# RWKV core: turning rows and making gates inside the block substitution, four masks moved behind it, one bank for the joins' y

## What is computed

```
def step(state, inp):
    r_t, w_t, k_t, v_t, kk_t, a_t = inp
    sa = jnp.einsum('bhij,bhj->bhi', state, -kk_t)
    state = (state * w_t[:, :, None, :]
             + sa[..., :, None] * (kk_t * a_t)[..., None, :]
             + v_t[..., :, None] * k_t[..., None, :])
    return state, jnp.einsum('bhij,bhj->bhi', state, r_t)
```

## Time and profile before

| what | value |
|---|---|
| runs | 1932.91, 1932.30, 1928.63 us; median 1932.3 |
| span of the profiled execution | 1938.0 us (its whole time is given by this span alone; no separate run time is shown) |
| mean granted PE clock of that execution | 0.981 |
| PE busy | 1867.0 us, 96% |
| DVE busy | 1620.9 us, 84% |
| ACT busy | 1144.5 us, 59% |
| `rwkv_core` in the trace | 574.2 to about 698 us |

### The profile page before, as it was taken

One profiled execution on the slowest core, in us unless ns is written; L12 is line 12 of the kernel. 1 busy time (PEld: TensorE's weight loads), 2 busy tenths in 40 slices (PEclk: granted clock), 3 DMA queues, 4 the chain that ended last, 5 costly groups with the idle time before them and its releaser, 6 DMA issues.

```text
span 1938.0 us, 27277 instructions
## 1 busy us (share of the span) xinstructions
PE 1867.0 (96%) x9408; PEld 1520.5 (78%) x9408; DVE 1620.9 (84%) x1752; ACT 1144.5 (59%) x1146; POOL 323.8 (17%) x336
## 2 busy tenths in 40 slices
PE   7999999999999998999999999999999999999997
PEld 6877777866777877888888888888888888888884
DVE  6877677944567577899999999999999999999996
ACT  4423344235563322577777777777777777777773
POOL 2101110020362510611111111111111111111110
PEclk9999999999997987999999999999999999999998
DMA  8545544041001233999999999999999999999994
GB/s 232 173 140 187 166 148 177 22 120 55 1 18 39 89 112 146 312 347 397 391 397 398 389 397 393 390 391 387 393 393 386 394 382 391 398 386 394 388 367 151
DMA packets 176817, 525.11 MB, mean 271 GB/s; under 512 B 30754, under 2 KB 48242, under 8 KB 176754
## 3 DMA queue, kind: packets, MB, share of 16 engines
q1 hardware_dynamic: 152722, 457.48, 62.2%
q0 software_dynamic: 21952, 66.78, 11.9%
q10 hardware_dynamic: 2080, 0.01, 0.1%
HBM read 499.08 MB, written 25.15 MB: 270 GB/s over the span
## 4 chain that ended last, share of the span: by engine, by line
PE 59%; DVE 2%; issue 0%; POOLq 0%; POOL 0%; DVEq 0%
PE banks L3614 54%; PE banks L3602 3%; PE banks L3608 1%; PE banks L3682 0%; DVE expert_weights L3962 0%; DVE x_tokens L3958 0%; DVE weights_lo L3753 0%; PE banks L3703 0%; DVE x_tokens L3969 0%; DVE x_tokens L3841 0%; PE banks L3740 0%; PE banks L3673 0%; DVE rows_lo L3783 0%; DVE member L3821 0%; DVE route_work L3863 0%
## 5 line engine op out<-in xcount | busy, mean ns | idle before, releaser
L3753 DVE TENSOR_TENSOR weights_lo<-expert_weights,weights_hi 128x2048 fp32r<-128x2048 f32 x384 | 876.9, 2289 | 65.3 <-ACT weights_hi L4000 62.3
L4000 ACT ACTIVATE weights_hi<-expert_weights 128x2048 fp32r<-128x2048 f32 x384 | 738.7, 1926 | 264.4 <-PE banks L3614 252.2
L3614 PE MATMUL banks<-weights_hi,rows_hi 128*128 128x512 f32 x1024 | 319.2, 393 | 0.0
L3614 PE MATMUL banks<-weights_hi,rows_lo 128*128 128x512 f32 x1024 | 315.5, 389 | 0.0
L3614 PE MATMUL banks<-weights_lo,rows_hi 128*128 128x512 f32 x1024 | 273.8, 389 | 0.0
L3614 PEld LDWEIGHTS banks<-weights_hi,rows_hi 128*128 128x128 f32 x1024 | 189.8, 188 | 44.9 <-issue 7.3
L3614 PEld LDWEIGHTS banks<-weights_hi,rows_lo 128*128 128x128 f32 x1024 | 192.3, 188 | 40.5
L3614 PEld LDWEIGHTS banks<-weights_lo,rows_hi 128*128 128x128 f32 x1024 | 192.3, 188 | 39.9
L3614 PE MATMUL banks<-weights_hi,u_hi 128*128 128x512 f32 x512 | 161.0, 396 | 0.0
L3614 PE MATMUL banks<-weights_hi,u_lo 128*128 128x512 f32 x512 | 157.9, 390 | 0.0
L3614 PE MATMUL banks<-weights_lo,u_hi 128*128 128x512 f32 x512 | 136.9, 389 | 0.0
(11 more groups left out here) (620 smaller groups left out, 2696.6 us busy)
## 6 DMA issues: line engine op xcount, KB each, us to landing
expert_weights<-in_exp_w SPq DMA_DIRECT2D x384, 1024.0 KB, 10.5
enter_rows<-in_ada_w POOLq DMA_DIRECT2D x24, 1024.0 KB, 6.5
w_in_landing<-in_w_in SPq DMA_DIRECT2D x16, 384.0 KB, 3.4
second_landing<-in_w_in SPq DMA_DIRECT2D x12, 512.0 KB, 3.7
x_tokens<-in_x SPq DMA_DIRECT2D x8, 512.0 KB, 7.2
w_in_landing<-in_w_in SPq DMA_DIRECT2D x8, 512.0 KB, 3.6
rwkv_room<-in_w_o SPq DMA_DIRECT2D x8, 512.0 KB, 6.4
w_in_landing<-in_w_in SPq DMA_DIRECT2D x12, 256.0 KB, 5.1
```

Of the source, the lines that this page charges most:

```text
L3614: last = nc.tensor.matmul(c.banks[:, bank + n, :], left[:, 2 * q + kk, :], right[:, q, kk * FF + n * 512:kk * FF + (n + 1) * 512], start=s ...
L3753: nc.vector.tensor_tensor(w_lo[:, ch % SPLIT, :], c.raw[:, ch % RAW if place is None else place, :], w_hi[:, ch % SPLIT, :], ALU.subtract) ...
L4000: nc.scalar.activation(w_hi[:, ch % SPLIT, :], c.raw[:, ch % RAW if place is None else place, :], ACT.Copy).then_inc(hi_ready.sem, 1)
```

## The change

- PE's order is written anew. Rows of b (`turn_rows` 4 to 7) come behind `times_values(0)`, rows of k (8 to 11) behind `times_values(1)`, the gates of tiles 0 and 1 behind these, those of tiles 2 and 3 between `times_values(2)` and `(3)`. Then come k products 4 to 7 in one piece and `times_values(4)` and `(5)`.
- `mask(4)` to `mask(7)` stand behind the substitution on DVE.
- The values of the last tile (units 6 and 7) are made inside the joins: `last_values(0)` behind y of step 0, `last_values(1)` behind y of step 1, 8 matmuls each; ACT copies their results at the same steps.
- y of both halves goes to bank 0 and is copied by one ACT operation of 128x256; `y` is stored without gaps.
- Banks of the turned rows, gates and values change, with the waits that go with them. The number of matmuls does not change; ACT has 8 copies less (one y copy per step instead of two).

```
-    turn_bank = lambda n: 6 + n % 2 if n < TT else 4 + n % 4
+    turn_bank = lambda n: 6 + n % 2 if n < TT else n % 4
+    gate_bank = lambda t: 4 + t % 2
+    value_bank = lambda t, k: (6 + k, 6 + k, 4 + k, 5 - 2 * k)[t]
...
                 pool.wait_ge(gains_in.sem, 32)
+                pool.wait_ge(k_ready.sem, units)
...
                     if i < 3:
                         pe.wait_ge(b_masked.sem, 5 + i)
+                    elif i == 5:
+                        pe.wait_ge(g_taken.sem, TT)
+                    elif i in (4, 6):
+                        pe.wait_ge(rows_copied.sem, 3 * TT)
                     else:
                         pe.wait_ge(k_masked.sem, i - 2)
...
-                    pe.wait_ge(k_masked.sem, g + 1)
+                    pe.wait_ge(k_masked.sem, g + 1 if t < 2 else 6)
...
+                def last_values(k):
+                    if k == 0:
+                        pe.wait_ge(mv_copied.sem, TT - 1)
+                    of_values(units - 2, k)
+                    of_values(units - 1, k).then_inc(mv_done.sem, 1)
...
-                for g in range(units):
-                    if g + 4 < units:
-                        k_products(g + 4)
-                    times_values(g)
-                pe.wait_ge(mv_copied.sem, TT)
-                pe.wait_ge(k_masked.sem, units)
-                for n in range(TT, 3 * TT):
+                times_values(0)
+                for n in range(TT, 2 * TT):
                     turn_rows(n)
+                times_values(1)
+                for n in range(2 * TT, 3 * TT):
+                    turn_rows(n)
+                gates(0)
+                gates(1)
+                times_values(2)
+                gates(2)
+                gates(3)
+                times_values(3)
+                for i in range(4, units):
+                    k_products(i)
+                times_values(4)
+                times_values(5)
...
                         if i == 0:
-                            pe.wait_ge(g_taken.sem, TT)
+                            pe.wait_ge(k_masked.sem, units)
+                        if i == 2:
+                            pe.wait_ge(mv_copied.sem, TT)
...
-                            last = nc.tensor.matmul(c.banks[high, 2, n * 64:(n + 1) * 64], nt[high, g, h, high], X0[high, g, h, high],
+                            last = nc.tensor.matmul(c.banks[high, 0, n * 64:(n + 1) * 64], nt[high, g, h, high], X0[high, g, h, high],
                                                     start=True, stop=True)
                         last.then_inc(y_ready.sem, 1)
+                        if i < 2:
+                            last_values(i)
...
-                        nc.scalar.activation(y[low, i % 2, :, low], flat_heads(c.banks[low, 0, 0:256]), ACT.Copy)
-                        nc.scalar.activation(y[high, i % 2, :, high], flat_heads(c.banks[high, 2, 0:256]), ACT.Copy).then_inc(y_copied.sem, 1)
+                        nc.scalar.activation(y[:, i % 2], flat_heads(c.banks[:, 0, 0:256]), ACT.Copy).then_inc(y_copied.sem, 1)
+                        if i < 2:
+                            mv(TT - 1, i)
...
-                    if 8 <= i < 20 and i % 3 == 2:
-                        mask(4 + (i - 8) // 3)
...
+                for i in range(4, units):
+                    mask(i)
```

More of the change, by code:

```diff
@@ L2906, in turn_rows @@
                         pe.wait_ge(b_masked.sem, units)
-                    if n >= TT + 4:
+                    if n == TT:
+                        pe.wait_ge(k_masked.sem, 4)
+                    elif n >= TT + 4:
                         pe.wait_ge(rows_copied.sem, n - 3)
@@ L2929, in k_products, with of_values, gates @@
                     last.then_inc(k_ready.sem, 1)
+                def of_values(g, k):
+                    t, q = step_of(g)
+                    for h, f, j, n in heads_of(q):
+                        last = nc.tensor.matmul(c.banks[:, value_bank(t, k), h * 64:(h + 1) * 64], kv_mat[:, g % 4, k, n, :],
+                                                v_tok[:, t, h * 64:(h + 1) * 64], start=True, stop=True)
+                    return last
                 def times_values(g):
                     t, q = step_of(g)
-                    pe.wait_ge(k_masked.sem, g + 1)
+                    pe.wait_ge(k_masked.sem, g + 1 if t < 2 else 6)
                     if g == 0:
                         pe.wait_ge(rows_copied.sem, TT)
-                    elif q == 0:
+                    elif q == 0 and t == 1:
                         pe.wait_ge(mv_copied.sem, t)
[L2940 to L2945, removed]
+                    of_values(g, 0)
+                    of_values(g, 1).then_inc(mv_done.sem, 1)
+                def last_values(k):
[3 more added lines that the diff above has]
+                    of_values(units - 1, k).then_inc(mv_done.sem, 1)
+                def gates(t):
+                    if t == 0:
+                        pe.wait_ge(k_masked.sem, 4)
+                    if t >= 2:
+                        pe.wait_ge(g_taken.sem, t - 1)
+                    nc.tensor.matmul(c.banks[:, gate_bank(t), :], gate["inputs"][:, t * P:(t + 1) * P], gate["weights"][:], start=True,
+                                     stop=True).then_inc(g_ready.sem, 1)
                 for i in range(3):
@@ L2981, in outputs @@
                         last.then_inc(o_ready.sem, 1)
[L2983 to L2986, removed]
+                pe.wait_ge(mv_copied.sem, 2)
                 for i in range(-2, units + 5):
@@ L3044, in _ @@
                             g, q = step_of(i - 1)
-                            nc.tensor.matmul(c.banks[low, 1, n * 64:(n + 1) * 64], y[low, (i - 1) % 2, n, low],
+                            nc.tensor.matmul(c.banks[low, 1, n * 64:(n + 1) * 64], y[low, (i - 1) % 2, n, :],
                                              inverse[low, g, 4 * q + n, low], start=True, stop=True)
-                            nc.tensor.matmul(c.banks[high, 4, n * 64:(n + 1) * 64], y[high, (i - 1) % 2, n, high],
+                            nc.tensor.matmul(c.banks[high, 4, n * 64:(n + 1) * 64], y[high, (i - 1) % 2, n, :],
                                              inverse[high, g, 4 * q + n, high], start=True, stop=True)
@@ L3057, in _ @@
                             lower = nc.tensor.matmul(c.banks[low, 2, n * 64:(n + 1) * 64], inverse[low, g, 4 * q + n, low],
-                                                     y[low, (i - 1) % 2, n, low], start=True, stop=True)
+                                                     y[low, (i - 1) % 2, n, :], start=True, stop=True)
                             if n == 3:
@@ L3120, in _, with mv, take_gates @@
                 nc.scalar.activation(latent["roots"], latent["sums"], ACT.Sqrt).then_inc(latent_roots.sem, 1)
[L3122 to L3126, removed]
+                def mv(t, k):
+                    act.wait_ge(mv_done.sem, 2 * t + 2 if t < TT - 1 else 2 * t + 1 + k)
+                    last = nc.scalar.activation((m0v, o_part)[k][:, t, :], c.banks[:, value_bank(t, k), :], ACT.Copy)
+                    if k:
+                        last.then_inc(mv_copied.sem, 1)
+                def take_gates(t):
+                    act.wait_ge(g_ready.sem, t + 1)
+                    nc.scalar.activation(scale_row[:, t, :], c.banks[:, gate_bank(t), :], ACT.Copy).then_inc(g_taken.sem, 1)
                 def root(t, heads=slice(0, RH), more=0):
@@ L3135, in _ @@
                     act.wait_ge(blocks_out[t].sem, 16 * B)
-                for t in range(TT):
-                    mv(t)
-                for n in range(TT, 3 * TT):
+                for n in range(TT, 2 * TT):
+                    copy_rows(n)
+                mv(0, 0)
+                mv(0, 1)
+                for n in range(2 * TT, 3 * TT):
                     copy_rows(n)
                 for t in range(TT):
-                    act.wait_ge(g_ready.sem, t + 1)
-                    nc.scalar.activation(scale_row[:, t, :], c.banks[:, t, :], ACT.Copy).then_inc(g_taken.sem, 1)
+                    take_gates(t)
+                for t in (1, 2):
+                    mv(t, 0)
+                    mv(t, 1)
                 for i in range(-2, units + 5):
```

2 lines of the change are left out of this document (1 added, 1 removed).

## The result

The changed kernel takes **1938.7 us** in the median of 13 executions (1932.0 to 1946.2), the kernel before 1932.9 beside it (13 executions, 1928.6 to 1936.8): 1.003 times as long, 95% interval 1.0015 to 1.0044. The forecast of 1938.8 holds to 0.1 us. The traces show two reasons for the loss, one forecast and one not; that together they give the forecast's figure is luck, as the part on the prediction shows.

A forecast was written before the change was run, and what follows sets the result against it. It took DVE's substitution as the bound to 618.6 us, then PE, then both nearly equally in the joins. Low-clock terms 4.9 + 1.0 + 0.6 gave +6.5 us on the median 1932.3: 1938.8, range 1927.5 to 1944.0.

The forecast's parts named there:

- the gap: PE idle ahead of k product 7, waiting for mask 4: some 6 us, taken to bring the clock to 0.50.
- done at 609.1: PE's transposes, values, gates and three k products beside the substitution, from 592.10 on: sum 17.0 us.
- the clock holds: Rival: PE keeps its clock ahead of the joins; first group 4.1 us earlier, 1928.2 us; chance 0.16.
- I expect it back within about one such step: In the joins after the first group: slow steps cost +1.7 us each until the clock returns; a third taken, +0.6.
- early return: Rival: the clock returns during the transposes ahead of the first y; first group +0.3 us, 1932.6 us; chance 0.16.
- PEclk 0.50 ... through both `last_values`: Sign: low clock from the PE idle time's second half through the last tile's values, 16 rows about 3.4 us.
- 23 to 24 us behind the last substitution step: Sign: where the joins' first group should start in the changed profile, against 13.7 us before.
- That execution lies 5.7 us above the median: Whole-kernel step carrying the forecast from the profiled execution, 1938.0 us, to the median of the runs, 1932.3.
- POOL's wait: POOL's new wait, for k product 7: met long before its scale work is done, so nothing.
- ACT's single copy: Joins' y copied in one operation saves ACT 0.38 us a step: nothing, at most 2.2 us gained.
- SP's scatter: SP's DMAs of the inverses move up with the substitution's earlier end; tile 0 lands at about 620.0.
- one bank for y costs PE its pairs: Rival: the joins' y halves run one after another, 3.2 us on top, 1942.0 us; chance 0.07.

The follow-up runs named there:

- after_look3: The changed kernel as it is, profiled once more to catch a long execution; 1946.1 us.
- y_one_bank: The kernel before with only the joins' y in one bank and one copy of 128x256; 1933.1 us, ratio 1.0002.
- after_again: The changed kernel as it is, profiled a second time; 1934.6 us.
- after_look1: The changed kernel as it is, one more profile to compare the length of the low-clock stretch; 1933.4 us.
- after_look2: The changed kernel as it is, one more profile looking for a long execution; 1931.2 us.
- masks_in: The changed kernel with masks 4 to 7 back between steps of the substitution, all else kept; 1938.0 us, ratio 1.0023 to before.
- fill_gap: The changed kernel plus 9 unread 128x512 matmuls between k products 6 and 7; 1930.4 us, ratio 0.9990 to before.
- two_two: The changed kernel with masks 4 and 5 back inside the substitution, values of units 6 and 7 ahead of the joins, 7 unread matmuls; 1932.9 us, ratio 1.0004 to before.

## Why the prediction was right, and where it was not

**The mechanism held up to the joins, in all five profiles.** The substitution ended 4.8 us earlier (23.2 against 27.9), mask 4 at 24.55 us behind the first operation (forecast: 615.1, which is 24.6). The clock fell in the gap each time. K product 7 took 2.08 (forecast 2.3, by doubling 1.14), and the joins' first transposes follow the values of units 4 and 5 8.9 us after k product 7 starts (forecast for the values' end 9.1).

**The gap was mis-sized.** Forecast some 6 us, measured 8.1 to 8.4. The step was "done at 609.1", 18.6 us behind the substitution's first operation; PE was done at 16.3. The work that the sum put at 17.0 us took 15.2, each part a little less: the 32 transposes 3.5 and not 4.2, three `times_values` 5.3 and not 5.8, the gates 3.5 and not 3.6, three k products in one piece 2.9 and not 3.4. It also began half a us earlier. The longer gap would have gone against "the clock holds", which no profile showed.

**The likeliest path was not the likeliest.** The sum from the joins on, "I expect it back within about one such step", describes after_look3 closely: first group at 46.7, +4.8 against 41.8 in the forecast's base (forecast +4.9); last group +6.9 (forecast +6.5 with the slow steps, of which there were nearly two and not a third of one); span 1944.2 where the sum on the profiled execution gave 1944.5. But four of five profiles are the rival "early return", with 41.5 to 42.2 and so -0.3 to +0.4 (its forecast +0.3). I had given it 0.16 and the forecast 0.49. The prediction's own signs say the same: "PEclk 0.50 ... through both `last_values`" and a first group "23 to 24 us behind the last substitution step" hold in after_look3 (23.5) alone; in the other four the group comes 18.4 to 19.0 us behind it.

**The shift to the median was wrong in kind.** "That execution lies 5.7 us above the median" took the profile of before as an ordinary execution with a constant added. It was not one: a stretch at 0.50 in its tail, 674.66 to 691.72, made the tail 43.0 us, against 37.6 in the other profile of that kernel and 36.6 in y_one_bank. Only 9 of 111 executions of before are at 1937 us or more. Leaving this tail out was right for before; the changed kernel has it in two of five profiles. The 5.7 us also compares a span with times: every run's time is about 1.9 us over its span, so the execution lay some 7.6 above the median. The forecast, median plus 6.5, does not hang on that.

**So why is the median 5.8 us up?** An estimate from the rows above: a low clock through the joins costs about 7 us (71.8 - 64.9), one in the tail about 6 (42.2 against some 36.5). Executions under 1937 have neither (after_again, after_look1, after_look2: 1934.6, 1933.4, 1931.2), those between one (the first profile, 1940.2, with the tail), those over 1942 both (after_look3, 1946.1; the profile of masks_in, span 1942.6, has both too). With 8 of 28 at 13 and 8 at 6.5 that is (104 + 52) / 28 = 5.6 us; for before, (13 + 8 x 6.5) / 111 = 0.6. The difference, 5.0, is most of the 5.6 us between the means (1938.5 and 1932.9). The three classes are set by time, so this only checks that the two prices suffice; the granted clock of each run, which falls class by class without overlap, supports it but does not say in which stage the clock was lost. The median of 1938.7 is thus no typical path: it lies among the executions that, by this estimate, lost the clock once. The forecast was one path at +6.5 for every execution; what was measured is a mixture of paths at about nothing, 6.5 and 13 us, whose middle fell on it. So the agreement to 0.1 us is luck, while the gap, the fall of the clock and the slower work behind it are not. fill_gap, which takes the gap away, turns +5.4 us over before in its batch into -2.6.

**The other steps.** POOL's wait and ACT's single copy at nothing: no row speaks against it, and the joins' 23.0 us in y_one_bank show it for the copy. SP's scatter was not quite at nothing: it starts 3.5 to 3.9 us behind the issue of its write in the five profiles, against 2.7 before, but PE came to the joins' transposes later still. The rival "one bank for y costs PE its pairs" falls by y_one_bank. By the quotation of the Trainium skill ("PSUM — Partial Sum Buffer", section "PSUM bank collisions raise a hardware error") these pairs would not have run side by side; the rows above show them 0.01 us apart. The rule of the Trainium skill that the higher clock does not engage for transposes ("TensorE: Matmul & The Clock Gate", section "Part 4: PE-mode transpose") would have ruled the early return out. It did not decide here: in three of five profiles the clock was back before or as the first y began (in the first at 627.09, with y at 627.83), and PE had run only values and transposes since k product 7.

**What stays open.** Why the clock returns early in one execution and late in another with the same rows ahead of it, and why the tail should lose it more often in the changed kernel, as the estimate has it: no run tells that apart. What the executions at 1937 to 1942 lost, and where, is seen in one trace only. No run moves the rows and gates alone, or `last_values` alone.

## What to carry to other kernels

Before moving work out of a DVE-bound stretch, look at what PE does at its end: a stretch shortened by 4.8 us brought nothing, because PE waited 8 us for the last mask and came out of it at half the clock, with work to do that had been covered before. If such a gap can't be closed by real work, a few matmuls whose result nobody reads can be worth as much time as they take: here the kernel with 8 us of them was 8 us faster than without, though not faster than the kernel before by more than this measurement can tell. And check whether the profiled execution is a typical one, stage by stage, before its numbers are carried over to the median of the runs.

## What the runs showed of the hardware

- With the same rows ahead of it to 0.2 us, the granted clock came back after 13.7 us in one execution and after 30.7 in another. The times of that one program span 1931 to 1947 us; this stretch and the one in the tail are most of the difference between two profiles of it (11.3 of 14.8 us, after_look2 and after_look3).
- A gap of 1.63 us on PE was followed by a fall of the clock within 1 us (two_two, 611.16 and 612.03); gaps of 0.52, 0.98 and 0.92 us in fill_gap's profile, the first of them behind 8 us of 128x512 matmuls, were not.
- Two matmuls of 64x64 on different row halves start 0.01 us apart when both write the same PSUM bank, as they do in two banks (y_one_bank, 627.64 and 627.65; before, 630.16 and 630.17).
